# TensorE's step order in the sparse and the latent attention: values, scores, turning in place of values, turning, scores

## What is computed

```python
# latent attention: 8 heads, blocks of 128 queries, only keys up to the block's end
logits = einsum('bhqd,bhkd->bhqk', q_nope[q0:q1], k_nope[:q1]) \
       + einsum('bhqd,bkd->bhqk', q_rope[q0:q1], k_rope[:q1])
probs  = masked_softmax(logits * scale, mask)
out    = einsum('bhqk,bhkd->bhqd', probs, v[:q1])

# sparse attention: 8 heads in 2 groups, three softmaxes of each query
p_c = softmax(where(m_c, q @ kc, NEG)) * m_c      # 31 compressed blocks
p   = softmax(where(m,   q @ ks, NEG))            # selected blocks (all 8, as 512/64 = 8 < 16)
pw  = softmax(where(mw,  q @ kw, NEG))            # window of 512, here the causal triangle
o   = g[0] * (p_c @ vc) + g[1] * (p @ vs) + g[2] * (pw @ vw)
```

## Time and profile before

| | us |
|---|---|
| median of 3 runs | 3465.77 |
| the runs | 3465.70, 3465.77, 3466.93 |
| span of the profiled execution | 3464.9 |
| PE busy | 3340.3 (96% of the span) |
| PEld busy | 2696.5 |
| DVE busy | 1814.4 |
| ACT busy | 1294.8 |

### The profile page before, as it was taken

The page is one execution under the profiler, slowest core; times in us unless marked ns, Lnnn a source line. Parts: engine busy times, 40 slices in busy tenths (PEclk is TensorE's granted clock), DMA queues, the critical chain, the costliest instruction groups (busy, mean ns, idle before and its releaser), DMA issues.

```text
span 3464.9 us, 46862 instructions
## 1 busy us (share of the span) xinstructions
PE 3340.3 (96%) x19963; PEld 2696.5 (78%) x19963; DVE 1814.4 (52%) x3053; ACT 1294.8 (37%) x2160; POOL 116.1 (3%) x210
## 2 busy tenths in 40 slices
PE   7999989999999999999899999999999989999998
PEld 5878756888888888887568888888888756788887
DVE  5565664577656665654754533353334475453333
ACT  4232565335434422234543322332223354342222
POOL 0000000010000010100000000000000000000000
PEclk9999999999999999999999999999999999999999
DMA  3110013464444265643112222322333311223231
GB/s 139 39 50 24 31 43 110 161 220 142 153 157 151 90 241 195 244 139 101 32 55 86 97 96 94 98 92 98 97 98 112 105 38 49 86 85 97 98 97 67
DMA packets 100544, 364.08 MB, mean 105 GB/s; under 512 B 11632, under 2 KB 11696, under 8 KB 99696
## 3 DMA queue, kind: packets, MB, share of 16 engines
q1 hardware_dynamic: 75888, 272.14, 23.6%
q0 software_dynamic: 24448, 88.95, 7.8%
HBM read 358.94 MB, written 2.10 MB: 104 GB/s over the span
## 4 chain that ended last, share of the span: by engine, by line
PE 86%; DVE 8%; ACT 4%; issue 1%; DMA 0%; POOL 0%; DVEq 0%; ACTq 0%; POOLq 0%
PE ps_run L435 85%; PE ps_run L781 1%; DVE wl L1890 1%; DVE nrm L1897 1%; ACT nrm L1171 1%; DVE HL L1897 1%; ACT wh L1171 1%; ACT nP L1171 0%; DVE nst L2565 0%; DVE ug L1890 0%; DVE AL L1890 0%; DMA vec<-vec 0%; ACT HH L1171 0%; DVE dP L2258 0%; DVE nrm L1890 0%
## 5 line engine op out<-in xcount | busy, mean ns | idle before, releaser
L435 PE MATMUL ps_run<-HH,wh 128*128 128x512 f32 (+1 forms) x2720 | 1064.8, 391 | 17.8 <-DVE wl L1890 10.5
L435 PE MATMUL ps_run<-HH,wl 128*128 128x512 f32 (+1 forms) x2720 | 1038.4, 382 | 0.0
L435 PE MATMUL ps_run<-HL,wh 128*128 128x512 f32 (+1 forms) x2720 | 1037.8, 382 | 0.0
L1890 DVE TENSOR_TENSOR wl<-st,wh 128x1024 fp32r<-128x1024 f32 x511 | 624.9, 1224 | 733.9 <-ACT wh L1171 733.8
L1171 ACT ACTIVATE wh<-st 128x1024 fp32r<-128x1024 f32 x511 | 537.3, 1054 | 708.4 <-PE ps_run L435 703.4
L435 PEld LDWEIGHTS ps_run<-HH,wh 128*128 128x128 f32 x2720 | 512.9, 189 | 127.5 <-DVE wl L1890 8.5
L435 PEld LDWEIGHTS ps_run<-HL,wh 128*128 128x128 f32 x2720 | 513.5, 189 | 100.0 <-issue 5.5
L435 PEld LDWEIGHTS ps_run<-HH,wl 128*128 128x128 f32 x2720 | 512.8, 189 | 100.1
L435 PE MATMUL ps_run<-AH,wh 128*128 128x512 f32 (+1 forms) x1167 | 443.6, 380 | 2.1 <-DVE wl L1890 2.1
L435 PE MATMUL ps_run<-AH,wl 128*128 128x512 f32 (+1 forms) x1167 | 441.2, 378 | 0.0
L435 PE MATMUL ps_run<-AL,wh 128*128 128x512 f32 (+1 forms) x1167 | 441.2, 378 | 0.0
(11 more groups left out here) (408 smaller groups left out, 3344.2 us busy)
## 6 DMA issues: line engine op xcount, KB each, us to landing
st<-wst SPq DMA_DIRECT2D x511, 512.0 KB, 3.3
mb<-ada POOLq DMA_DIRECT2D x144, 512.0 KB, 4.4
cw<-cw POOLq DMA_DIRECT2D x4, 1024.0 KB, 7.0
X<-xT SPq DMA_DIRECT2D x8, 256.0 KB, 10.2
X<-xT POOLq DMA_DIRECT2D x8, 256.0 KB, 5.1
out<-X SPq DMA_DIRECT2D x8, 256.0 KB, 2.8
kc<-kc POOLq DMA_DIRECT2D x1, 1139.5 KB, 7.4
mb<-cond POOLq DMA_DIRECT2D x2, 512.0 KB, 5.1
```

The costliest lines, as they stand in the source:

```text
L435: i = self.e.matmul(out, lhsT, rhs, start=start, stop=stop, skip_group_check=True)
L1890: self.e.tensor_tensor(out, a, b, op).then_inc(*self.w.done(*points))
```

## The change

In both `pipeline` calls of class `Pe` the stages turning and scores change places, with their offsets. The offsets themselves stay: values run four steps behind, turning three, scores none. The mask belongs to the scores. ScalarE's, VectorE's, GpSimd's and SyncE's streams keep the same instructions in the same order; no instruction is added or taken away.

```diff
@@ class Pe, mla @@
-        finish(pipeline(16, (values, both(turn), scores), (4, 3, 0)))
+        finish(pipeline(16, (values, scores, both(turn)), (4, 0, 3)))
@@ class Pe, nsa @@
-        yield from pipeline(36, (values, turn, scores), (4, 3, 0))
+        yield from pipeline(36, (values, scores, turn), (4, 0, 3))
```

## The result

The changed kernel took 3506.9, 3515.1, 3517.1 and 3520.8 us (median 3516.1), the kernel before 3466.4 beside it: a ratio of 1.0132 [1.012, 1.0144]. The profiled execution is the one of 3506.9, its span 3504.9: the profiles tell of 40.0 us, the medians of 49.7. The other three runs have a mean granted clock of 0.981 to 0.982, the profiled one 0.986. The first view is its page's head and part 1, then TensorE's waits over the whole span (total, times, longest), to be set beside the earlier trace rows.

A forecast was written before the change was run, and what follows sets the result against it. TensorE was taken as the bound, busy 3340.3 of 3464.9 us. Latent 5.0 plus two layers of 12.1 + 4.6 made 38.4 us, with 2 for the clock +40: 3506 us, 1.2% slower, range 3485 to 3530.

The forecast's parts named there:

- the 2 us for the clock: Whole kernel: more idle time puts more stretches at the lower clock, 2 us added to the sum of the loops.
- One sign of being wrong: Latent loop: the forecast is wrong if this loop isn't about 5 us longer than its 59.
- Latent, +5.0: Latent loop: bare copies cost 8.3 us, less 2.7 for three vanished waits and 0.6 at end and start.
- the lower bound: Latent loop: only +1 us if its end's slow clock is avoided because the 1.89 us idle time splits into shorter ones.
- Sparse to step 18, 12.1 a layer: Sparse steps that stall already: late turning and copy delay everything behind them; 12.1 us a layer, bounds 7 to 19.
- Sparse from step 19, 4.6 a layer: Sparse steps without stalls: waits for the scores' bank return where a slab is split; 4.6 us a layer, bounds 0 to 6.
- TensorE's own work stays as it is: Both attention loops: apart from some 27 us of waits, all is TensorE's own work, which the change leaves as it is.
- The first: Sparse loops: copy not in the chain, a stalled step costs its turning alone; +19 us, 3485 us; chance 0.12.
- The second: Clock falls in the latent loop and oftener in the sparse ones: 15 us more, 3521 us; chance 0.13.
- The third: Both loops: faster, if copies were hidden and earlier scores shorten the waits; -11 us, 3455 us; chance 0.03.
- The two effects: Whole kernel: gain and loss cancel within 7 us, with latent +5 and sparse at nearly nothing; chance 0.03.
- The rule of the prediction on turnings and the clock: Latent loop: transposes don't count as clock activity, so a turning with bare waits on either side is as good as idle.

The follow-up runs named there:

- nsa_only: Kernel before with the new order (scores ahead of the turning) in the sparse attention alone: 3503.0 us, ratio 1.0095.
- mla_again: mla_only with no edit, run again for a profile of another execution: 3482.1 us.
- nsa_to18: Kernel before with the new order in steps 0 to 18 of either sparse attention only: 3499.8 us, ratio 1.0088.
- nsa_from19: Kernel before with the new order from step 19 on in either sparse attention only: 3473.8 us, ratio 1.0013.
- late_even: Kernel before with the new order in the even sparse steps from step 19 on only: 3468.1 us, ratio 0.9997.
- late_odd: Kernel before with the new order in the odd sparse steps from step 19 on only: 3468.2 us, ratio 1.0003.
- dbl_after: Kernel before with the new order in the latent attention alone, and ScalarE making every copy of a turned tile there twice: 3512.3 us, ratio 1.0127.
- mla_only: Kernel before with the new order in the latent attention alone: 3477.2 us, ratio 1.0016.
- both_early: Kernel before, TensorE's order kept; sparse maxima and exponentials in the step of their scores, latent copies ahead of exponentials on ScalarE: 3473.7 us, ratio 1.0014.
- after: The changed kernel itself, new order in both attentions, against the kernel before: median 3516.1 us, ratio 1.0132.
- after_again: The changed kernel with no edit, run again for a profile of another execution: 3505.3 us.

## Why the prediction held, step by step

The forecast was 3506 us, 1.2% slower; the median is 3516.1 and the profiled run 3506.9. Direction and mechanism held. That the profiled run comes within 1 us is luck in part. Set against its terms, the latent loop took 2.5 us less than forecast, the sparse steps to 18 took 5.4 more than their term and the 2 us for the clock together (31.6 against 26.2), those from 19 on 4.3 less (4.9 against 9.2), and 1.7 us were added outside the loops, where nothing was forecast. One sign of being wrong that it named also showed: the latent loop is not about 5 us longer but 2.5. Of the terms:

- **Latent, +5.0.** The waits grew by 5.5 us, and the four bare copies are within 0.02 of the forecast 0.53, 0.64, 0.74 and 0.85. The loop grew by 2.5 only, as TensorE's busy time in it fell by 3.1. Some 1.1 of that is the 0.37 of each of three rounds, which the forecast did not have: it took TensorE's own work as unchanged. Most of the rest is at the end, where the lower bound stood: its clock went from 0.58 to 0.87. Whether the split of the long wait did that is not shown, for nsa_only, with the old order in this loop, has 0.74 there. In other executions the clock takes more than that: mla_again's loop is 8.1 longer than before's.
- **Sparse to step 18, 12.1 a layer.** The chain was the forecast one, link by link: second copy to end 2.3 us behind the start of the scores of step 11 (measured 1694.71 - 1692.43 = 2.28), scores of step 12 to move by 1.1 (measured 1.01). Waiting grew by 11.7 a layer, all idle time by 12.0 and 13.3. The time grew by 16.5 and 15.1, and the difference, 4.5 and 1.9, is busy time of the same matmuls at a lower clock, net of what the order gives back (next point). This is the term that was mis-sized, by 3 to 4 us a layer, and the step at fault is the sum's separate 2 us for the clock in both layers, which measured 6.4 here. In nsa_to18 the granted clock is 0.83 over 1629 to 1722 us and 0.93 over 1722 to 1770, before 0.91 and 1.00. The rows of the changed kernel have such places behind the waits that grew:

```profile
1675.72 1.90 PE L435 MATMUL ps_run<-kw,qT 64*128 64x512 f32 x4 [2.37 <-ACT nP L1171]
...
1737.53 0.39 PE L435 MATMUL ps_run<-cmpb,identb 128*128 128x128 bf16 x2 [2.76 <-ACT nP L1171]
1737.85 1.92 PE L435 MATMUL ps_run<-kcr,qT 64*128 64x31 f32 x16
```

  Four products of 512 columns take 1.13 at full clock and 1.90 here.
- **Sparse from step 19, 4.6 a layer.** Waits grew by 4.4. The one at step 26 was to be 1.46:

```profile
1784.29 1.13 PE L435 MATMUL ps_run<-kw,qT 64*128 64x512 f32 x4 [1.40 <-ACT nP L1171]
```

  The time grew by 2.4 only. The step that failed is the sentence that TensorE's own work stays as it is. A turning followed by scores holds TensorE longer than one followed by dense products. First the scores of before that follow the turning of six pieces in the earlier trace rows by 0.81 us (it started at 1763.04), then such a turning of the changed kernel, with the dense work 0.58 behind its start:

```profile
1763.85 1.13 PE L435 MATMUL ps_run<-kw,qT 64*128 64x512 f32 x4
```

```profile
1785.47 0.82 PE L781 MATMUL ps_run<-kc,nP 128*128 128x128 f32 x6
1786.05 0.47 PE L435 MATMUL ps_run<-HH,wh 128*128 128x512 f32 x1
```

  In the timelines of before and of nsa_from19 over 1720 to 1840 us the mean distances from a turning to what follows are 0.37, 0.59, 0.81 and 1.02 us for 2, 4, 6 and 8 pieces ahead of scores, and 0.14, 0.36, 0.61 and 0.82 ahead of dense products: 0.20 to 0.23 less each. The mask ahead of the turning takes 0.12 where it took 0.09 ahead of dense work. That is 0.19 gained in each of 17 steps, some 3.2 us a layer, against waits of 4.4 and idle time of 4.9 on the mean. It fits late_even, whose loops are 0.9 and 1.0 shorter than before's with 8 such steps. late_odd, with 9 of them and 1.2 us more waiting a layer, has loops 0.7 longer, which it does not explain.
- **The rivals.** The first (copy not in the chain, 7 us a layer in the sparse loops) fell with nsa_to18, whose idle time grew by 12.0 and 13.3, and with the rows of steps 11 and 12; dbl_after shows the copy in the chain of the latent loop. The second (clock) is real in part. In the profiled changed kernel the granted clock over the two sparse loops is 0.92 and 0.93, before 0.96 and 0.95, but its busy time in them changed by +1.4 and -1.6 us only, since the shorter sequences offset it. In the latent loop the clock cost nothing in two profiles of the changed kernel and 7 us in one of two of mla_only. It is the likely reason why the median lies over the sum. The third asked for a hidden copy; none was. The two effects did not cancel.

What stays open is where the upper runs of the changed kernel spend their 10 us, and with it some 7 us that the two halves of the change, run alone, do not add up to.

## What to carry to other kernels

A product that feeds a copy should stand as far ahead of the copy's reader as the order allows, and ahead of work that nobody waits for; its place on TensorE is also the place of everything queued behind the copy on ScalarE. When two engines' orders are interleaved by hand, follow one wait through all queues before swapping two stages in one of them. Moving the exponential forward removed most of that wait here (21.3 to 6.4 us in both_early) but put others behind it, so the order of ScalarE and VectorE has to be costed with the dense work that shares them.

## What the runs showed of the hardware

- Scores (64*128 in the rows) that follow a turning (128*128) start 0.20 to 0.23 us later than dense products (128*128) do, with 2, 4, 6 or 8 pieces (above). A sparse step of before changes between such forms four times (values to turning, to scores, to mask, and dense work to the next values), the new one three times, since mask, turning and dense work have one form. The Trainium skill, TensorEngine Tiling (Array Packing), Key Properties, says that changing the tiling mode drains TensorE. By that rule, if the forms of the rows are such modes, the step with one change less gains something; the trace agrees, and its number is 0.22 us for this one, less 0.03 at the mask. It does not show that every change of form costs. The compressed turnings have a form of their own (128*31), yet dense products start 0.79 us after eight of them, no later than after eight of the others, and scores after 0.99.
- The granted clock of a loop with a regular idle time in each step: 1.00 over 500 to 535 us with 0.5 to 0.8 us in steps of 2.5 to 4.5 us (after, after_again, mla_only), 0.76 in another execution of the same instructions (mla_again), 0.65 and then 0.50 with 1.1 to 2.1 us (dbl_after). In the last, 11.4 us of longer waits made the loop 38.9 us longer than mla_only's.
- The rule of the prediction on turnings and the clock stays undecided. Turnings with bare waits behind them left the clock at 1.00 in three profiles and did not in a fourth.
